# Scan of a hybrid GDN / RWKV / attention layer: corner products as 32x32 blocks, state copy and decay of the RWKV state on GpSimd

## What is computed

```python
# gated delta rule, per chunk (4 heads of 128)
t_inv = triangular_solve(lower + eye, eye)          # inverse of a unit lower triangular 64x64
v_new = val_i - kc_i @ s
o     = q_i @ s + attn_i @ v_new
s     = s * exp(gl_i) + kt_i.T @ v_new

# RWKV-7, per token (8 heads of 64), done here per chunk with the same kind of 64x64 inverse
s   = s * w_t + (s @ -kk_t) (kk_t*a_t)^T + v_t k_t^T
out = s @ r_t
```

## Time and profile before

| | us |
|---|---|
| median of 3 runs | 2008.74 (2006.83 to 2012.97) |
| profiled execution, whole | 2008.84 |
| its span, first to last instruction | 2007.1 |
| scan stage in it | about 790 to 976 |
| one chunk in the middle of the scan | 10.78 |

### The profile page before, as it was taken

How to read it: one execution, slowest core, us unless ns; L and a number is a source line. 1 busy time by engine, 2 the same in 40 slices (tenths; PEclk the granted TensorE clock), 3 DMA queues, 4 the chain that set the end, 5 groups by cost and what they waited for, 6 DMA issues and landing times.

```text
span 2007.1 us, 29418 instructions
## 1 busy us (share of the span) xinstructions
PE 1934.2 (96%) x11744; PEld 1562.7 (78%) x11744; DVE 1034.9 (52%) x1363; ACT 588.4 (29%) x952; POOL 545.0 (27%) x336
## 2 busy tenths in 40 slices
PE   8999999999999999999889999999999999999994
PEld 6777787677788887888667687788888888888883
DVE  2747643864459601777676429324242424242437
ACT  3434533334221211656421311222111212122112
POOL 1221122211122313344143824321212222121203
PEclk9999999999999998999999999999999999999997
DMA  6345672336553582686553632121212121211102
GB/s 161 62 101 129 165 171 81 84 93 167 137 145 100 133 235 85 188 239 202 180 172 116 205 105 61 35 63 31 63 31 63 31 63 32 62 38 56 48 5 84
DMA packets 339847, 211.86 MB, mean 106 GB/s; under 512 B 166140, under 2 KB 310140, under 8 KB 337696
## 3 DMA queue, kind: packets, MB, share of 16 engines
q1 hardware_dynamic: 264176, 156.38, 28.1%
q10 hardware_dynamic: 75568, 54.04, 9.4%
HBM read 151.27 MB, written 59.06 MB: 105 GB/s over the span
## 4 chain that ended last, share of the span: by engine, by line
PE 45%; DVE 3%; POOL 1%; DMA 1%; ACT 0%; issue 0%; SPq 0%; DVEq 0%; ACTq 0%
PE b_ps L154 11%; PE b_ps L155 11%; PE b_ps L156 11%; PE f_ps L154 4%; PE f_ps L155 4%; PE f_ps L156 4%; DMA o_raw<-in_w_out 1%; DVE l_stats L2277 1%; POOL x1lo L1764 1%; DVE y L2289 0%; DVE y L2274 0%; PE f_ps L1845 0%; POOL wo_lo L1770 0%; PE f_ps L1807 0%; POOL x1lo L1756 0%; PE f_ps L1882 0%
## 5 line engine op out<-in xcount | busy, mean ns | idle before, releaser
L154 PE MATMUL bank<-xhi,w_hi 128*128 128x512 f32 x976 | 393.2, 403 | 2.3 <-POOL w_lo L433 1.5
L155 PE MATMUL bank<-xlo,w_hi 128*128 128x512 f32 x976 | 385.8, 395 | 0.0
L156 PE MATMUL bank<-xhi,w_lo 128*128 128x512 f32 x976 | 385.7, 395 | 0.0
L433 POOL TENSOR_TENSOR w_lo<-w_raw,w_hi 128x1024 fp32r<-128x1024 f32 x61 | 167.9, 2753 | 600.3 <-ACT w_hi L799 600.3
L2249 DVE TENSOR_TENSOR bw_raw<-bw_raw,b_ps 128x512 f32<-128x512 f32 x42 | 28.9, 688 | 388.4 <-PE b_ps L156 380.1
L154 PEld LDWEIGHTS bank<-xhi,w_hi 128*128 128x128 f32 x976 | 183.7, 188 | 48.4 <-POOL w_lo L433 3.4
L156 PEld LDWEIGHTS bank<-xhi,w_lo 128*128 128x128 f32 x976 | 183.4, 188 | 44.5
L155 PEld LDWEIGHTS bank<-xlo,w_hi 128*128 128x128 f32 x976 | 183.6, 188 | 43.8 <-issue 1.7
L2257 DVE TENSOR_TENSOR y<-y,f_ps 128x512 f32<-128x512 f32 x320 | 200.5, 684 | 0.5
L1792 POOL TENSOR_TENSOR bw_split<-ff_raw_down,ff_hi_down 128x1024 fp32r<-128x1024 f32 x22 | 53.3, 2422 | 526.7 <-ACT ff_hi_down L2050 526.7
L154 PE MATMUL f_ps<-ff_hi_down,ff_hhi 128*128 128x512 f32 x352 | 142.3, 404 | 3.6 <-DVE ff_hlo L2268 3.6
(11 more groups left out here) (324 smaller groups left out, 3443.7 us busy)
## 6 DMA issues: line engine op xcount, KB each, us to landing
w_raw<-in_w_in ACTq DMA_DIRECT2D x61, 512.0 KB, 4.4
op<-opnd SPq DMA_DIRECT2D x16, 1152.0 KB, 5.5
u<-work ACTq DMA_DIRECT2D x68, 256.0 KB, 4.0
b_gate<-u SPq DMA_DIRECT2D x24, 512.0 KB, 3.6
ff_raw_gate<-in_ffn_gate SPq DMA_DIRECT2D x22, 512.0 KB, 4.0
ff_raw_up<-in_ffn_up SPq DMA_DIRECT2D x22, 512.0 KB, 5.4
ff_raw_down<-in_ffn_down SPq DMA_DIRECT2D x22, 512.0 KB, 5.9
opnd<-work SPq DMA_DIRECT2D x20, 512.0 KB, 5.7
```

What stands on the lines that cost most here:

```text
L154: pe.matmul(out, w_hi, x_hi, start=first, stop=False)
L155: pe.matmul(out, w_hi, x_lo, start=False, stop=False)
L156: return pe.matmul(out, w_lo, x_hi, start=False, stop=last)
L433: pool.tensor_tensor(w_lo[b][:, :, :], w_raw[b][:, :, :], as_f32(w_hi[b][:, :, :]), ALU.subtract).then_inc(w_lo_done, 1)
```

## The change

1. The tiles `inv` and `join`, the function `place_inverse`, the clearing of both tiles and the early placing of chunk 0 are removed.
2. PE multiplies the 32x32 blocks straight from the loaded tiles: the corner `corner` on 32 partitions with the diagonal inverse `packed`, 32 columns. The result `y` has 32 partitions per head and 32 columns; the second product takes it to the upper 32 partitions. The number of matmuls stays 12 and 12. `ps_y` and `ps_z` get columns of their own in the bank.
3. ACT copies `y` by two instructions of 32 partitions instead of one of 128.
4. `zt` is cleared once at the start of the scan. POOL copies the diagonal blocks of each chunk into it (four copies of 32x192, in `product`), DVE copies the corner (two copies of 32x192) instead of the addition over 128x384.
5. The decay of the RWKV state into `sv` goes from DVE to POOL, in two halves, each waiting for its half of `s_sum`. In POOL's list it stands in `state(c)` ahead of `s_dec`, followed by a wait for its own completion.
6. The waits are adapted: `zt_done` counts two per chunk, PE waits for `inv_done` ahead of L1294, SP waits for `inv_done` ahead of a reload.

```diff
-def place_inverse(pool, c, tiles, join_done, inv_done):
-    op, ar, sv, wv, packed, corner, inv, join = tiles
-    b, d = c % 2, c % DEEP
-    for k in (0, 64):
-        pool.tensor_copy(join[b][k:k + 32, :, NB:2 * NB], corner[d][k:k + 32, :, :]).then_inc(join_done, 1)
-    pool.wait_ge(join_done, c * 2 + 2)
-    for q in range(4):
-        rows, t0 = slice(32 * q, 32 * q + 32), NB * (q % 2)
-        pool.tensor_copy(inv[b][rows, :, :, t0:t0 + NB], packed[d][rows, :, :, :]).then_inc(inv_done, 1)
...
+        upper = [slice(64 * e, 64 * e + NB) for e in range(2)]
+        lower = [slice(64 * e + NB, 64 * e + 2 * NB) for e in range(2)]
...
-                        last = pe.matmul(ps_y[h, u, :], join[b][h, u, :], inv[b][h, 0, u, :], start=True, stop=True)
+                        last = pe.matmul(ps_y[lower[e], u, :], corner[d][upper[e], u, :], packed[d][upper[e], 0, u, :], start=True, stop=True)
...
-                        last = pe.matmul(ps_z[h, u, :], y[b][h, u, :], inv[b][h, 1, u, :], start=True, stop=True)
+                        last = pe.matmul(ps_z[upper[e], u, :], y[b][lower[e], u, :], packed[d][lower[e], 1, u, :], start=True, stop=True)
...
-                act.activation(y[b][:, :, :], ps_y, ACT.Copy).then_inc(y_done, 1)
+                for e in range(2):
+                    act.activation(y[b][lower[e], :, :], ps_y[lower[e], :, :], ACT.Copy).then_inc(y_done, 1)
...
-                dve.tensor_tensor(zt[b][:, :, :], ps_z, inv[b][:, 1, :, :], ALU.add).then_inc(zt_done, 1)
+                for e in range(2):
+                    dve.tensor_copy(zt[b][upper[e], :, NB:2 * NB], ps_z[upper[e], :, :]).then_inc(zt_done, 1)
...
-                dve.wait_ge(s_sum_done, c * 2 + 2)
-                for e in range(2):
-                    h = rwkv_rows(e)
-                    dve.tensor_tensor(sv[(c + 1) % DEEP][h, of(e), :], s_sum[b][h, :, :],
-                                      plast[h, :].rearrange("p (j c) -> p j c", j=4)[:, :, c:c + 1].to_broadcast([64, 4, C]), ALU.mult).then_inc(s_rw_done, 1)
...
-                if c:
-                    place_inverse(pool, c, tiles, join_done, inv_done)
+                if c >= 2:
+                    pool.wait_ge(mm_w, c - 1)
+                for e in range(2):
+                    for k, half in enumerate((upper[e], lower[e])):
+                        pool.tensor_copy(zt[b][half, :, k * NB:(k + 1) * NB], packed[d][half, 1, :, :]).then_inc(inv_done, 1)
...
             def state(c):
                 b, d = c % 2, c % DEEP
                 pool.wait_ge(tok_done, c + 1)
+                for e in range(2):
+                    h = rwkv_rows(e)
+                    pool.wait_ge(s_sum_done, c * 2 + e + 1)
+                    pool.tensor_tensor(sv[(c + 1) % DEEP][h, of(e), :], s_sum[b][h, :, :],
+                                       plast[h, :].rearrange("p (j c) -> p j c", j=4)[:, :, c:c + 1].to_broadcast([64, 4, C]), ALU.mult).then_inc(s_rw_done, 1)
+                pool.wait_ge(s_rw_done, c * 2 + 4)
                 pool.wait_ge(s_g_done, c * 2 + 2)
                 pool.tensor_tensor(s_dec[b][:, :, :], s_g[b][:, :, :], egl_bc[:, :, c:c + 1].to_broadcast([P, GH, GD]), ALU.mult).then_inc(dec_done, 1)
```

More of the change, by code:

```diff
@@ L260, in scan_tiles @@
     packed, corner = loads("inv_packed", [2, NPAIR, NB]), loads("inv_corner", [NPAIR, NB])
-    inv, join = ([sb(f"{name}{b}", [P] + shape) for b in range(2)] for name, shape in (("inv", [2, NPAIR, C]), ("join", [NPAIR, C])))
-    return op, ar, sv, wv, packed, corner, inv, join
+    return op, ar, sv, wv, packed, corner
 def load_chunk(sp, c, tiles, opnd, xinv, landed, inv_landed):
-    op, ar, sv, wv, packed, corner, inv, join = tiles
+    op, ar, sv, wv, packed, corner = tiles
     b, row = c % DEEP, opnd[c]
@@ L387, in project_and_prepare @@
         inv_landed, inv_cleared, inv_stored = sem("inv_landed"), sem("inv_cleared"), sem("inv_stored")
-        early_landed, early_inv, early_cleared, early_join, early_placed = (sem("early_" + n) for n in ("landed", "inv", "cleared", "join", "placed"))
+        early_landed, early_inv = (sem("early_" + n) for n in ("landed", "inv"))
         inv_step = [sem(f"inv_step{k}") for k in range(2)]
@@ L434, in _ @@
             local.sweep(pool)
[L435 to L443, removed]
         @block.sync
@@ L1148, in scan_and_attend @@
         local.enter_context(nc.sbuf_tensor("scan_tiles", [P, sum(math.prod(t.shape[1:]) for group in tiles for t in group)], F32))
-        op, ar, sv, wv, packed, corner, inv, join = tiles
+        op, ar, sv, wv, packed, corner = tiles
         causal, attn = two("causal", [8, C]), two("attn", [2, 2, C])
         tok_g = two("tok_g", [2, 2, GD])
-        y, zt = two("y", [NPAIR, C]), two("zt", [NPAIR, C])
+        y, zt = two("y", [NPAIR, NB]), two("zt", [NPAIR, C])
         r_rw, r_g, w_g = two("r_rw", [4, C]), two("r_g", [2, GD]), two("w_g", [2 * GD])
@@ L1157, in scan_and_attend @@
         ps_a, ps_yz, ps_at = bank("ps_a", [2, C]), bank("ps_yz", [512]), bank("ps_at", [512])
-        ps_y = ps_z = ps_yz[:, 0:NPAIR * C].rearrange("p (u s) -> p u s", u=NPAIR)
+        ps_y, ps_z = (ps_yz[:, n * NPAIR * NB:(n + 1) * NPAIR * NB].rearrange("p (u s) -> p u s", u=NPAIR) for n in range(2))
+        upper = [slice(64 * e, 64 * e + NB) for e in range(2)]
+        lower = [slice(64 * e + NB, 64 * e + 2 * NB) for e in range(2)]
         ps_vt = ps_yz[:, NPAIR * C:]
@@ L1170, in scan_and_attend @@
         mm_m, mm_a, mm_y, mm_z, mm_r, mm_w, mm_s, mm_o = (sem("mm_" + n) for n in "mayzrwso")
-        masked, attn_done, inv_done, join_done, tok_done, y_done, zt_done = (
-            sem(n) for n in ("m_masked", "attn_done", "inv_done", "join_done", "tok_done", "y_done", "zt_done"))
+        masked, attn_done, inv_done, tok_done, y_done, zt_done = (
+            sem(n) for n in ("m_masked", "attn_done", "inv_done", "tok_done", "y_done", "zt_done"))
+        zt_cleared = sem("zt_cleared")
         r_rw_done, r_g_done, w_done, s_sum_done, s_rw_done, dec_done, s_g_done, o_done = (
@@ L1521, in _ @@
         def _(pool):
-            pool.sem_inc(join_done, 2)
-            pool.sem_inc(inv_done, 4)
             pool.memset(keys[:, :, 0:C], 0.0).then_inc(padded, 1)
             pool.memset(values[:, 0:C], 0.0).then_inc(padded, 1)
+            for b in range(2):
+                pool.memset(zt[b][:, :, :], 0.0).then_inc(zt_cleared, 1)
+            pool.wait_ge(zt_cleared, 2)
             def product(c):
```

23 lines of the change are left out of this document (12 added, 11 removed).

## The result

The changed kernel takes **2028.1 us** (median of 4 runs, 2026.1 to 2029.1) against 2009.2 (2006.8 to 2013.0) for the kernel before, run beside it: a ratio of 1.0094, with a 95% interval of 1.0081 to 1.0106. It is slower, as forecast, but by about 19 us instead of 7, and outside the range. The profiled execution has a span of 2027.3 us (2007.1 before) at a granted clock of 0.984.

The account below looks back on a forecast made before the run. PE's list bounds the kernel before at 10.78 us per chunk; a chain through POOL's list then sets 11.33, so 13 steps add 7.3 to 2008.84, making 2016.1, given as 2016 us, range 2010 to 2020.5.

Parts of the forecast that it names:

- the second chain: From `s_sum` through POOL's `sv`, `s_dec`, copies and `tok_g`, then `r_g`, ACT and L1343: the longer chain, 11.33 us per chunk.
- The fourth sign: At L1282: some 0.5 to 0.9 us idle before it, ended by DVE's `s_g`, would show the forecast right.
- PE stays the bound: Rival: PE's list still sets the period, 10.20 us per chunk, about 2001 us in all; chance 0.06.
- instructions on different partitions overlap: Rival: POOL's instructions on different partitions overlap, giving 10.91 us per chunk, +1.8, 2010.6 us; chance 0.09.
- Only the first chain binds: Rival: the path `s_sum`, `sv`, `s_dec`, `s_g` to L1282 sets 11.06 us per chunk, +3.8, 2012.6 us; chance 0.11.
- the small blocks aren't shorter: Rival: PE's corner products keep a pitch of 0.84, giving 11.49 us per chunk, +9.4, 2018.2 us; chance 0.06.
- POOL is slowed by DVE: Rival: `sv` on POOL takes 1.14, giving a period of 12.47 us and 2031 us; chance 0.04.
- the half of `sv`: On POOL, one 64x256 half of the decay taken as 0.57 us, with bounds 0.45 and 0.69.
- Behind the last L1343 nothing changes but POOL: At the scan's end: POOL's L1549 ends about 974.8, next block starts at 975.96, 1.1 us of cover left.
- I take 0 with 0.8 either way: Ahead of the 13 counted steps: shorter first corner products and first late `tok_g` give 0, with 0.8 us either way.
- `y` at nothing: ACT's two copies add less than 0.38 us ahead of the exponentials, covered by L1282's longer wait for `s_g`.
- The corner blocks: On PE, the second block's pitch falls from 0.84 to 0.42 us; the first product gives at most 0.16 at L1305.

Follow-up runs that it names:

- e4: Changed kernel with POOL scaling the next chunk's `tok_g` ahead of `sv`, `s_dec` still behind `sv`; 2020.7 us, ratio 1.0061.
- e2: Changed kernel with `s_dec` ahead of the two halves of `sv` in POOL's list; 2019.2 us, ratio 1.0052.
- e1: Changed kernel with the 89 semaphore clears moved from the end of POOL's list into chunk 0; 2024.7 us, ratio 1.0082.
- e3: Changed kernel with the decay into `sv` back on DVE, behind `s_g`; 2015.2 us, ratio 1.0033.
- e5: Changed kernel with POOL's order `s_dec`, next chunk's copies and `tok_g`, then `sv`, and semaphore clears in chunk 0; 2012.2 us, ratio 1.0025.
- e10: e5 with `y` copied by one ACT instruction over 128 partitions, unwritten rows zeroed once; 2004.7 us, ratio 0.9980.
- e7: Kernel before with only `sv` moved to POOL, in two halves behind `s_dec`, the placing copies and `tok_g`; 2010.9 us, ratio 1.0015.
- e9: e7 with the semaphore clears in chunk 0; 2008.6 us, ratio 0.9998.

## Why the prediction was wrong in size

**Right: who ends the step.** Three of the waits that the prediction named are there, DVE's L1395 for `s_dec`, L1384 for `tok_g`, and L1324 for ACT's L1493 (0.36 per chunk, forecast 0.2 to 0.3). e4 took the second chain out alone, and e2 shortened both. The fourth sign, 0.5 to 0.9 of idle time ahead of L1282 that `s_g` ends, isn't there in that form: L1262 has 0.3 (4.1 over 14), "issue" by the profile, because L1331 ahead of it is itself stretched to 1.17 by its waits for ACT's scaling. "PE stays the bound" (2001) and "instructions on different partitions overlap" (2010.6) are out: after's two halves take 1.31 and its four copies 1.53, twice 0.62 and four times 0.34 with gaps between. "Only the first chain binds" is out by e4, "the small blocks aren't shorter" by the pitch of 0.49, and "POOL is slowed by DVE" by a half of `sv` at 0.62 instead of 1.14. The rule of the Trainium skill (GPSIMD Engine Reference, section 2.1) on cores that start the next instruction when their share is done can't be seen in these rows.

**Mis-sized: the second chain.** Forecast 11.33, measured 11.56, which is +3.0 over 13 steps. Its parts:

| part | forecast | measured |
|---|---|---|
| first half of `s_sum`, reaction of POOL | 0.57 | 0.56 |
| two halves of `sv` | 1.17 | 1.31 |
| `s_dec` with the gap ahead of it | 1.19 | 1.13 |
| gap, four copies, gap, `tok_g`, gap | 2.80 | 2.88 |
| `r_g` to L1324 | 1.35 | 1.44 |
| L1324 to the next L1391 | 4.25 | 4.24 |

The failing choice was the half of `sv`: "I take 0.57, since both readings are equally near", and it was 0.618, the reading with the fixed part kept. Here half the columns cost 59% of the whole (0.618 of 1.05). With the gap that is 0.14 of the 0.23 per chunk; the path from `r_g` over ACT was read 0.09 too short, and what the copies and `tok_g` took more (0.08) `s_dec` took less (0.06).

**Wrong: the end.** "Behind the last L1343 nothing changes but POOL", and "L1549 with 2.68 ends at about 974.8". This step of the prediction failed: it let POOL's list end with L1549, and put what is queued behind it at nothing without a reason. There were 89 clears, 6.5 us, and the trace of before had 92 of them at the same place. This is the largest miss, +5.4 in the span, and e1 shows it.

**Too tight: the start.** "I take 0 with 0.8 either way"; the trace has +1.9. The step from chunk 0 to chunk 1 was 12.15 and is 13.86, and the next one, which the sum of 13 steps left out though it has the same chain in it, was 11.10 and is 11.57. (The scan itself began 0.3 sooner in after. In e1 and e4 it began 2 us sooner still and chunk 2 came at 824.8 and 824.0, with first steps of 14.04 and 13.86, so a single +1.9 is in part scatter.) The granted clock may have had a part in the first step; windows of before (first) and after (second):

```profile
808.00:811.00 3.00, 2.40 (x26) 1.43 (x22) 2.47 (x6) 2.56 (x9) 1.13 (x2) 1.00 0.46 95
811.00:814.00 3.00, 2.93 (x56) 2.48 (x56) 1.82 (x6) 0.80 (x3) 2.65 (x6) 1.00 0.97 376
```

```profile
808.00:811.00 3.00, 1.67 (x14) 1.00 (x14) 1.70 (x6) 2.56 (x10) 2.61 (x6) 0.99 0.60 172
811.00:814.00 3.00, 3.00 (x38) 2.67 (x36) 0.61 (x2) 0.92 (x3) 0.27 (x1) 0.50 1.01 339
```

After three microseconds in which PE was busy for 1.67, the granted clock was 0.50 (1.2 GHz) for the next three, with 38 instructions in them where before has 56. In e2 and e3 no such drop stands there and the first step is long all the same (12.82 and 13.25), so the clock isn't the whole of it.

**Not foreseen, and open: the stalls.** In chunks 5 and 9 PE stops inside or around L1242, "issue" by the profile, that is for nothing that it shows:

```profile
910.40 0.53 PE L1242 MATMUL ps_yz<-inv_packed,inv_corner 32*32 32x32 f32 x21
911.88 0.25 PE L1242 MATMUL ps_yz<-inv_packed,inv_corner 32*32 32x32 f32 x3 [0.95 <-issue]
```

They cost 1.6 us here. Such stalls are in e1, e2, e4, e5 and e10 too and once in e7 (0.44 at L1271), which has the old products, but not in e3. It would be natural to blame full DMA engines, and the windows don't bear it out: their share is 0.32 in the stall before 911.88 and 0.47 in the one before 864.73, while chunks without a stall have windows at 1.07 (850 to 853) and 1.09 (900 to 903). The cause stays open.

**Right for now, but dangerous: `y` at nothing.** "I take it at nothing, because L1282 behind it will wait longer than this for `s_g` (below, 0.51); without that cover it would cost some 0.2 per chunk." In after the cover holds by the rows, though no run of after with one copy was made. With the order repaired it is gone, and the copies cost 0.48 per chunk (e5 against e10), not 0.2.

**The corner blocks** have a pitch of 0.49, forecast 0.42, not the 0.84 of the rival. These are 24 records in 0.49, 20 ns each, or 12 matmuls, 41 ns each. The Trainium skill (TensorE: Matmul & The Clock Gate, Part 1) has a floor of about 25 ns between the starts of two matmuls. Counted over 24 records, as the prediction did, that would be 0.60, and the trace is under it; counted over the 12 matmuls, that floor makes an estimate of 0.30, and the trace is above it. So the working with 24 records failed, and the rows don't speak against the floor. The first block gave about its forecast 0.16: L1286 starts 0.84 after `wv` (887.97 against 887.13) instead of 0.99. The second gave 0.35 of PE's time, but of both together only 0.16 per step reached the time, and that only in e10 (against e9).

**Read wrongly, without harm to the sum: the collision at L1417.** The prediction took 0.8 for each half of `sv` on DVE, 0.41 of it its own. The 1.60 of the earlier trace rows is a merged row. Timelines of before from 885.73 us and from 971.45 us show the second half alone, in a usual chunk and in the last one, where POOL has no `s_dec` beside it:

```profile
885.74 1.16 DVE L1417 TENSOR_TENSOR sv<-s_sum,plast 64x256 f32<-64x256 f32 x1
```

```profile
971.46 0.42 DVE L1417 TENSOR_TENSOR sv<-s_sum,plast 64x256 f32<-64x256 f32 x1
```

The first half took 0.41 in every chunk, the second 1.16, and it ended 0.28 after `s_dec` did (886.90 against 886.62). That is as if DVE's second half had stood still until POOL's `s_dec`, begun 0.21 before it, was done; the two were not slowed alike. The rival "POOL is slowed by DVE", at twice the time for each half, was priced from this wrong reading.

Put together: 7.3 forecast, 3.0 for the chain's terms, 5.4 for the clears, 1.9 for the start, 1.6 for the stalls and 1.0 for the rest make the 20.2 of the spans. The range was too narrow since it held the terms of the chain alone: even with `sv` at its upper bound (2019.2) it had no place for the ends.

## What to carry to other kernels

An operation that is moved to an idle engine costs by its place in that engine's list, not by its length: put it behind everything that another engine is about to need (one exchanged pair gave 10.94 instead of 11.56). When an engine ends later than before, follow its list to the very last instruction, semaphore clears too, which count as busy in no view. And splitting a copy by partitions saved nothing on ScalarE: one over all 128 partitions took as long as one over 32, so two small ones cost twice.

## What the runs showed of the hardware that I had not expected

- A semaphore clear on GpSimd comes every 74 ns (44 ns in the record); 89 of them are 6.5 us, enough to hold up a whole stage by 5.2.
- ScalarE copies 192 columns in 0.32 whether on 32 or on 128 partitions, and what stands behind is held up by more than the second copy's length in the record: from `w_g` to `at_vt` 1.10 pass with two and 0.50 with one.
- GpSimd and VectorE don't share a collision equally. With `sv` on VectorE beside `s_dec`, its second half took 1.16 instead of 0.42 and ended only after `s_dec`, while `s_dec` took 1.09 instead of the 1.05 that it takes with `sv` on GpSimd. Without the collision both halves take 0.86 on VectorE (the last chunk of before) and 1.31 on GpSimd.
